# Two transformer blocks on one core: the first part's shift taken from DVE to PE, and later parts' transposes spread over the matmuls

## What is computed

```
cs  = silu(c)                                   # c: 2048 values
mod = cs @ w_ada + b_ada                        # w_ada: 2048 x 12288
sh1, sc1, gt1, sh2, sc2, gt2 = split(mod, 6)
h    = rmsnorm(x, g_pre_mix) * (1 + sc1) + sh1  # x: 256 x 2048
proj = h @ w_in                                 # w_in: 2048 x 11344
...                                             # attention, FFN, and a second block
```

## Time and profile before

| | |
|---|---|
| median of 3 runs | 2662.69 us (2661.63 to 2665.32) |
| the profiled execution | 2660.39 us, of which the span 2658.6 us |
| instructions in the span | 30389 |
| PE, DVE, ACT busy | 96%, 65%, 46% of the span |
| moved by DMA | 567.08 MB, mean 213 GB/s |

### The profile page before, as it was taken

One profiled execution on the slowest core, in us unless ns is written; L12 is line 12 of the kernel. 1 busy time (PEld: TensorE's weight loads), 2 busy tenths in 40 slices (PEclk: granted clock), 3 DMA queues, 4 the chain that ended last, 5 costly groups with the idle time before them and its releaser, 6 DMA issues.

```text
span 2658.6 us, 30389 instructions
## 1 busy us (share of the span) xinstructions
PE 2564.2 (96%) x12304; PEld 2123.1 (80%) x12304; DVE 1721.1 (65%) x2256; ACT 1211.1 (46%) x1764; POOL 5.9 (0%) x15
## 2 busy tenths in 40 slices
PE   4999998999998999999999989999999999999998
PEld 3787787887786888888888868878778888888887
DVE  6895878878886776556556564546656465564555
ACT  3634444533346534434434455455554444443443
POOL 0000000000000000000000000000000000000000
PEclk8999999999999999999999999999999999999999
DMA  8994345688985776555555535533445555555553
GB/s 324 366 355 155 120 160 188 253 336 326 339 328 197 260 292 229 191 190 184 196 188 181 201 135 189 190 127 143 178 155 190 190 184 196 189 181 200 185 196 142
DMA packets 80442, 567.08 MB, mean 213 GB/s; under 512 B 8976, under 2 KB 9104, under 8 KB 15664
## 3 DMA queue, kind: packets, MB, share of 16 engines
q1 hardware_dynamic: 79200, 558.09, 57.4%
q0 software_dynamic: 1104, 7.07, 0.7%
HBM read 563.02 MB, written 2.10 MB: 213 GB/s over the span
## 4 chain that ended last, share of the span: by engine, by line
PE 82%; DVE 11%; ACT 3%; DMA 2%; issue 2%; DVEq 0%; SPq 0%; ACTq 0%
PE ps L879 18%; PE ps L876 18%; PE ps L877 18%; PE ps L920 15%; PE ps L922 8%; DVE wl L1503 4%; DVE ACC L1522 3%; DMA raw<-stream_in 2%; ACT wh L1158 1%; PE ps L933 1%; PE ps L1102 1%; DVE TMP L1626 1%; ACT M L1283 1%; DVE M L1630 1%; PE ps L1078 0%
## 5 line engine op out<-in xcount | busy, mean ns | idle before, releaser
L1503 DVE TENSOR_TENSOR wl<-raw,wh 128x1024 fp32r<-128x1024 f32 x851 | 1003.2, 1219 | 575.2 <-ACT wh L1158 574.8
L1158 ACT ACTIVATE wh<-raw 128x1024 fp32r<-128x1024 f32 x851 | 852.4, 1049 | 742.2 <-PE ps L879 566.4
L920 PE MATMUL ps<-HT,wh 128*128 128x512 f32 x1792 | 634.0, 399 | 0.0
L876 PE MATMUL ps<-wh,U 128*128 128x512 f32 x1376 | 538.1, 391 | 0.0
L879 PE MATMUL ps<-wl,U 128*128 128x512 f32 x1376 | 536.4, 390 | 1.4 <-DVE wl L1503 1.4
L877 PE MATMUL ps<-wh,U 128*128 128x512 f32 x1376 | 535.6, 389 | 0.0
L922 PE MATMUL ps<-HT,wl 128*128 128x256 f32 x1792 | 503.5, 281 | 0.6 <-DVE wl L1503 0.6
L876 PE MATMUL ps<-wh,HT 128*128 128x512 f32 x1120 | 452.3, 404 | 18.0 <-ACT wh L1158 9.6
L879 PE MATMUL ps<-wl,HT 128*128 128x512 f32 x1120 | 447.3, 399 | 12.5 <-DVE wl L1503 12.3
L877 PE MATMUL ps<-wh,HT 128*128 128x512 f32 x1120 | 443.1, 396 | 0.0
L920 PEld LDWEIGHTS ps<-HT,wh 128*128 128x128 f32 x1792 | 336.6, 188 | 82.8 <-DVE M L1867 0.2
(11 more groups left out here) (227 smaller groups left out, 1297.8 us busy)
## 6 DMA issues: line engine op xcount, KB each, us to landing
raw<-stream_in SPq DMA_DIRECT2D x497, 1024.0 KB, 4.8
raw<-stream_in SPq DMA_DIRECT2D x16, 896.0 KB, 7.2
raw<-stream_in SPq DMA_DIRECT2D x17, 640.0 KB, 6.3
raw<-stream_in SPq DMA_DIRECT2D x13, 512.0 KB, 3.9
M<-rows_in POOLq DMA_DIRECT2D x6, 1024.0 KB, 5.1
X<-x_in SPq DMA_DIRECT2D x2, 1024.0 KB, 7.4
y_out<-X SPq DMA_DIRECT2D x4, 512.0 KB, 2.7
CT<-consts_in POOLq DMA_DIRECT2D x1, 376.0 KB, 6.8
```

What stands on the lines that cost most here:

```text
L876: e.matmul(o, ah, H[:, c:c + bw], start=k == k0, stop=False)
L920: e.matmul(o[:, :], H[:, c], a.rearrange("p h n -> p (h n)"), start=k == 0, stop=False)
L1158: e.activation(H, raw[place[n][0]][:, c:c + w], ACT.Copy).then_inc(*hi.tick(p))
L1503: e.tensor_tensor(L, raw[place[n][0]][:, c:c + w], H.bitcast(F32), ALU.subtract).then_inc(*lo.tick(p))
```

## The change

- The shift of the first part is no longer summed on DVE. For each of its four transfers of a pair, PE makes four float32 matmuls (`row_vec`), with a column of `cs` as the weights and 256 columns of `w_ada` as the moving operand, which add up to one row of 256 values in bank 4. ACT copies the row (`row_copy`), and PE turns it to two columns with two matmuls by one 1; DVE sums only the 256 columns of scale. SP waits for both readers.
- DVE's sums of the first transfer, and PE's row of it, come ahead of the norm of x.
- After a part, only the first pair of the next part's `turnx` tasks is finished; the others are taken by the hooks, one in each weight block.
- The `w_ada` transfers of the third part stand beside the first 14 weight blocks of the second part, without the two gaps of before, so their column sums are due two blocks earlier.

```diff
-    beside(phase(1), columns, (1, 1, 1, 1, 1, 0, 1, 1, 1, 1, 1, 0, 1, 1, 1, 1, 0, 0))
+    beside(phase(1), columns, (1, 1, 1, 1, 1, 1, 1, 1, 1, 1, 1, 1, 1, 1, 0, 0, 0, 0))
...
-    add("xnorm")
-    add("xturn", 0)
-    add("xturn", 1)
-    for n in range(4):
-        ada(n)
-    colsum(3)
-    add("xhalves", 0)
+    def first_mods(pair, n0):
+        for n in range(n0, n0 + 4):
+            ada(n)
+            add("rowvec", n)
+            if n == 0:
+                add("xnorm")
+                add("xturn", 0)
+                add("xturn", 1)
+        add("rowcopy", n0 + 3)
+        colsum(n0 + 3)
+        add("xhalves", pair)
+
+    first_mods(0, 0)
     split(4)
...
-    for n in range(5, 9):
-        ada(n)
-    colsum(8)
-    add("xhalves", 1)
+    first_mods(1, 5)
...
         flush()
-        drain()
+        finish("turnx", X_TILES.index((PHASES[q + 1], 2)))
...
+                if events[m][0] == "p":
+                    e.wait_ge(*rowvec(m))
                 e.wait_ge(*read_last(m))
...
+            for t in range(4):
+                k = 4 * i + t
+                ins = e.matmul(bank[4][0:1, 0:256], VT[:, V_C + k:V_C + k + 1], raw[place[n][0]][:, 512 * t:512 * t + 256],
+                               start=k == 0, stop=k == 15)
+            ins.then_inc(*rowvec.tick(n))
...
+            if events[n][0] == "p":
...
+                e.wait_ge(*copied(("row", n)))
+                for j in range(2):
+                    e.matmul(bank[7][:, j:j + 1], FIRST_ROW[:, 128 * j:128 * j + 128], ONES[0:1, 0:1], start=True, stop=True)
+                e.wait_ge(*acc((n, 1)))
+                for j in range(2):
+                    ins = e.matmul(bank[7][:, 2 + j:3 + j], ACC[:, 128 * j:128 * j + 128], ONES[:, 0:1], start=True, stop=True)
...
+            e.wait_ge(*rowvec(n))
+            e.activation(FIRST_ROW, bank[4][0:1, 0:256], ACT.Copy).then_inc(*copied.tick(("row", n)))
...
+                if kind == "p":
+                    r = raw[place[n][0]][:, 512 * t + 256:512 * t + 512]
```

More of the change, by code:

```diff
@@ L586, in build @@
     ACC = sb("ACC", [128, 1792])
-    PB, PTB = ACC[:, 1024:1408], ACC[:, 1408:1792]
+    PB, PTB, FIRST_ROW = ACC[:, 1024:1408], ACC[:, 1408:1792], ACC[0:1, 512:768]
     ONES = sb("ONES", [128, 128])
@@ L607, in build @@
     gemm, turned, score, value = signal("gemm"), signal("turned"), signal("score"), signal("value")
-    colsum = signal("colsum")
+    colsum, rowvec = signal("colsum"), signal("rowvec")
     hi, evac_a, high, scaled = signal("hi"), signal("evac_a"), signal("high"), signal("scaled")
@@ L797, in acc_width @@
         kind, q, _ = events[n]
-        return {"p": 512, "a": 1024}.get(kind) or 256 * (PHASES[q + 1] - PHASES[q])
+        return {"p": 256, "a": 1024}.get(kind) or 256 * (PHASES[q + 1] - PHASES[q])
     def mods_key(n):
@@ L924, in tile, with row_vec @@
             free[i % 4] = [(evac_v, (name, i))]
+        def row_vec(n):
+            i = events[n][2]
+            if i == 0:
+                for s, k in free[4]:
+                    e.wait_ge(*s(k))
+            e.wait_ge(*silu("c"))
+            e.wait_ge(*arrived(n))
+            for t in range(4):
[3 more added lines that the diff above has]
+            ins.then_inc(*rowvec.tick(n))
+            free[4] = [(copied, ("row", n))]
         def column_sums(n):
             e.wait_ge(ones_set, 1)
+            if events[n][0] == "p":
+                for s, k in free[7]:
+                    e.wait_ge(*s(k))
+                e.wait_ge(*copied(("row", n)))
[4 more added lines that the diff above has]
+                    ins = e.matmul(bank[7][:, 2 + j:3 + j], ACC[:, 128 * j:128 * j + 128], ONES[:, 0:1], start=True, stop=True)
+                ins.then_inc(*colsum.tick((n, 1)))
+                free[7] = [(mods, mods_key(n))]
+                return
             if not by_rows(n):
@@ L1139, in tensor @@
                 column_sums(*what)
+            elif kind == "rowvec":
+                row_vec(*what)
             elif kind == "xturn":
@@ L1198, in x_turn, with row_copy @@
                              scale=RS[:, t:t + 1]).then_inc(*xq.tick((p, t)))
+        def row_copy(n):
+            if n > 3:
+                e.wait_ge(*colsum((3, 1)))
+            e.wait_ge(*rowvec(n))
+            e.activation(FIRST_ROW, bank[4][0:1, 0:256], ACT.Copy).then_inc(*copied.tick(("row", n)))
         def x_halves(p):
@@ L1476, in scalar @@
                 x_halves(*what)
+            elif kind == "rowcopy":
+                row_copy(*what)
             elif kind == "turn":
@@ L1551, in column_sums @@
                 k0, nt = (2 * col, 2) if kind == "p" else (PHASES[col], PHASES[col + 1] - PHASES[col])
-                take_shift(0, V_SH1, k0, nt, bank[4][:, 0:nt])
-                take_scale(1, V_SC1, V_GMIX, k0, nt, bank[4][:, nt:2 * nt])
+                b = bank[7 if kind == "p" else 4]
+                take_shift(0, V_SH1, k0, nt, b[:, 0:nt])
+                take_scale(1, V_SC1, V_GMIX, k0, nt, b[:, nt:2 * nt])
             elif part == 3:
```

## The result

| | before | changed |
|---|---|---|
| median | 2662.16 us (4 runs, 2661.37 to 2665.32) | 2646.32 us (4 runs, 2645.48 to 2648.35) |
| profiled execution, its span | 2660.39, 2658.6 us | 2645.48, 2643.7 us |

What follows compares the result with a forecast made beforehand. PE's matmuls were taken as the bound, busy 96% of the span. Gains of 2.9 (start), 0.8 and 7.2 us (ends of first and second part) less 0.4 (DVE) made 10.5 us: 2649.9 profiled, 2652 predicted as median, range 2645 to 2660.

Steps and rivals of the forecast that it cites:

- rival 5: Start: clock at 2.4 GHz from the first transposes on, PE goes on after second pair at about 44; 2645 us; chance 0.08.
- first pair: Start: with PE's row matmuls the first weight matmul comes at 29.7 us, 2.1 us sooner.
- second pair: Start: PE goes on behind the second pair at 49.5 us instead of 51.91, 2.4 us sooner, first pair's 2.1 included.
- shorter slow stretch: Behind the second pair: PE idles 4 us, not 11, so less slow pace; 0.5 of 2.4 us gained.
- end of the first part: PE's second wait for ACT to scale x shrinks from 1.1 to 0.3 us; gain 0.8 us.
- DVE in the second part: Sums beside 14 blocks instead of 16 leave DVE no idle time, banks may be freed late; 0.4 us lost.
- end of the second part: Matmuls between the transpose pairs leave 0.9 us of waits and 1.2 of slow pace; gain 7.2 us.
- behind D: Behind slab kiwi nothing moves, so the earlier gains reach the end unchanged; no term of its own.
- rival 1: Start: all 32 row matmuls stay at 1.2 GHz and cost 0.86 us each; 2664 us; chance 0.12.
- rival 2: Start: row matmuls' weight loads do not hide, up to 1.32 us each; slower, 2679 us; chance 0.05.
- Rival 3: Second part: DMA becomes the bound over its first 14 blocks, 9.1 us late; 2661 us; chance 0.05.
- Rival 4: End of the second part: pairs meet ACT's roundings, half of the 7.2 us stays as waits; 2656 us; chance 0.07.

Runs made afterwards that it cites:

- e7: Changed kernel with the second pair wholly on DVE, without row matmuls there: median 2648.23 us, 0.9949 of the kernel before.
- e2: Kernel before with finish() of the next pair in place of drain(), counts and start as before: median 2655.02 us, ratio 0.9974.
- e8: Kernel before run again, unchanged: median 2661.57 us, ratio 1.0001.
- e9: Changed kernel run again, unchanged: median 2647.92 us, 0.9945 of the kernel before.
- e1: Kernel before with only the new start (first part's shift by row matmuls), drain() and old counts kept: median 2655.73 us, ratio 0.9979.
- e12: Changed kernel with the second part's 14 column blocks beside its first 12 weight blocks: median 2653.16 us, 0.9961 of the kernel before.
- e10: Repeat of e6, the changed kernel with 128 columns on PE and 384 on DVE in the second pair: median 2646.09 us, 0.9935 of the kernel before.
- e11: Changed kernel with 128 columns on PE and 384 on DVE in both pairs: median 2643.99 us, 0.9925 of the kernel before.
- e3: Kernel before with only the second part's new counts, drain() and start as before: median 2655.04 us, ratio 0.9975.
- e4: Kernel before with finish() for drain() and the new counts, start as before: median 2653.19 us, ratio 0.9970.
- e6: Changed kernel with 128 columns on PE and 384 on DVE in the second pair: median 2644.18 us, 0.9936 of the kernel before.

## Why the prediction was right, and where its sum was off

The time, 2646.3, lies in the range, and faster was given 0.78. It lies only 1.3 us above the lower end, and the range reached down to 2645 for rival 5, whose mechanism did not come; that part was luck. The signs were right for the first pair, the ends of both parts and DVE, and wrong for two small terms. The terms stand against the traces so:

| term | forecast | measured | from |
|---|---|---|---|
| first pair (A) | -2.1 | -3.6 (middle of seven traces 27.80, of five with the old start 31.63: -3.8) | A |
| second pair | -0.3 | +0.9 (+0.2 to +1.2 in five traces) | B - A, e7 |
| shorter slow stretch | -0.5 | +0.4, within the spread between executions | C - B: 52.46, now 52.83 |
| end of the first part | -0.8 | -1.3 | S - C: 97.43, in e2 96.16 |
| DVE in the second part | +0.4 | +0.5 | S - C: e2 to changed, 96.16 - 10.88 = 85.28, now 85.76 |
| end of the second part | -7.2 | -9.3 | D - S: 42.83, now 44.40 - 10.88 = 33.52 |
| behind D | 0 | -2.5, of which -1.3 by the change | end - D, e8 and e9 |
| sum of the profiled executions | -10.5 | -14.9 | |

- **First pair.** Every duration was near, and three small ones were too high: the transposes 2.1 (measured 1.70), four of twelve rows at the slow pace (none: 5.34 for the twelve instead of 6.9), the column sums 1.4 (1.1). PE's first row matmul started at 13.41, when the transfer was in, 0.5 later than the 12.9 that I had. Row matmuls at 0.875 and 0.44 were forecast at 0.86 and 0.43.
- **Second pair.** The step "the 24 matmuls take 8.9 us as before" failed: 9.65 here (37.86 - 28.21), where the first two are faster, PE then waits 1.13 us for `wl`, and the slow pace follows all the same; 9.89 in e9, with a wait of 1.32. Where they start slow, they take 9.0 (e1). Worse, I compared the go-on with before as if DVE would still be done at 47.47; with A 3.6 us sooner DVE alone would have been done sooner too. e7 shows that: 20.13 both times. My sum put the second pair's share at 0.3 us of gain (2.4 less 2.1) and never asked whether the rows were needed there.
- **Slow stretch.** "PE now idles 4 us there, not 11, so the slow stretch should be shorter" is not borne out: 6.5 us behind the go-on instead of 5.6. Over all traces it is 5.2 to 7.8 us in the five with the old start, where PE idles 5.8 to 7.0 us ahead of its sums, and 5.6 to 6.9 in the nine others. The longer stretch of the changed kernel is therefore not shown to be an effect of the change either. In e7 PE idled 6.3 us ahead of its sums and C - B was the same 52.9.
- **End of the first part.** The wait fell from 1.07 to 0.24, as forecast (0.3). The other 0.4 us are PE's waits for DVE to free a bank: none in e2 between 123 us and S.
- **DVE** cost what I took, 0.4. e12 shows what lies beyond.
- **End of the second part** was the term mis-sized most. I left 0.9 for two waits, 1.2 for the slow pace, and 0.2. The waits are gone: with one or two roundings between the pairs ACT keeps up. The slow pace is a matter of the execution: with both parts of the change it is absent in six traces (D - C 130.1) and there in two (e10, e11: 131.8), so my 1.2 us was near what it costs where it comes (1.6) and, in the trace at hand, not paid. Without one of the parts it stood behind S in all five traces. Why it does so stays open; between e3 and e4 only `drain()` differs, well ahead of it.
- **Behind D** I wrote "Behind slab `kiwi` nothing moves" and put the term at nothing because no instruction moves there. The instructions are the same, but PE's waits for `wl` between 262 and 370 us behind D are gone, and that stretch is 1.3 us shorter in this trace, some 1.6 by the middles.

The rivals: 1 and 2 fell with the pace of the rows, 0.44 us with a new column of weights each; an unhidden load would show above 0.43. The Trainium skill (TensorE: Matmul & The Clock Gate, part 1) calls the slower clock the default, released by matmul activity; by that rule rival 1 fails, and the trace agrees: the rows behind the transposes took 0.44. Rival 3 fell: from 80 to 104 us DMA moved 412 GB/s, from 123 to 187.8 it moved 364, and e12 drew 373 where it waited, for DVE; no transfer is waited for. The Trainium skill (DMA: Bandwidth & Descriptors, "Where 436 GB/s comes from") bounds transfers from HBM at about 358 GB/s; the trace does not agree, 412 GB/s from 80 to 104 us. Rival 4 fell with the waits. Rival 5 names nearly the time measured, 2645, and is wrong all the same: the clock did not stay up, and PE went on at 49.26, not at 44. The 4.4 us by which the traces beat the sum (14.9 against 10.5) come from elsewhere, 2.5 of them from behind D.

So by the traces' own places the change is worth 2.3 to 2.9 us ahead of C, 10.1 between C and D, and 1.3 to 1.6 behind D: 13.7 to 14.6 in all. The medians say 15.8, 15.2 (e9) and 14.7 (e1 and e4). What stays between them is inside the interval of each. For the start alone 3.0 + 1.6 = 4.6 us stand against 6.1 by the median of e1 (interval 3.2 to 8.0).

## What to carry to other kernels

When work is shared out between two engines, redo the comparison at each place with the times that the change itself brings: the same split that, with the new place of the norm, gained 3.6 us in the first pair cost 0.2 to 1.2 in the second, and 128 columns instead of 256 turned that to a gain of 2.6 to 3.2 over leaving the pair to DVE (B - A 16.98 to 17.57 against 20.13 in e7). A task that runs long on one engine and short on another is best spread between the bound engine's own blocks, and there are two levers for it: how it is queued, and when its input is due; alone they gave 7.0 and 4.7 us of D - C, together 10.1. For effects of a few us in a kernel whose runs spread by 8, take fixed places of the trace and differences between them: D - C repeated to 0.06 us over six traces of five kernels, while the median of the kernel before moved by 2.3 between chips (2660.84 and 2663.14). And "the instructions do not move there" does not mean that the time does not: compare the stretch over several traces of each kind.

## What was not expected of the hardware

- The pace behind a group of one-column matmuls (the 28 records at S) falls in some executions of the same instructions and not in others: the sums take 3.04 us to the next matmul where they run fast throughout, 3.54 and 3.80 where the pace falls within them (e3, e8).
- The transposes behind the first four row matmuls ran mostly at 0.21 us in the changed kernel, e6 and e9, and at 0.11 for the most part in e1, e7, e10 and e12, with the same instructions ahead of them. A wandered by 1.5 us (27.37 to 28.84) over seven executions, mostly for this and for when the first transfer landed.
- A float32 row matmul with one column of weights costs 0.44 us for 256 columns and 0.23 for 128 at 2.4 GHz, and 0.875 and 0.43 (e11: four in 1.7 us) at 1.2 GHz, weight load included.
- In a stretch of unchanged instructions that begins 262 us behind D, the nine traces with row matmuls at the start took 107.05 to 107.47 us and the five without 108.34 to 108.98.
- Behind D one and the same program took 2411.45 and 2419.12 us, at no lower mean clock (0.99 and 0.989).
